# GLA values taken token by token, with the first adaLN block behind them

## The chip, the cores and the metric

The kernel runs on one core of one Trainium2 chip. The metric is the device time of one execution in microseconds; several runs are taken and their median is given. A profile is one execution recorded by the hardware profiler: its span goes from the first to the last instruction of that execution, and its rows name lines of the kernel (L863 is line 863).

The engines are called by their names and by the short forms of the profile: TensorE (PE for its matmuls, PEld for its weight loads), VectorE (DVE), ScalarE (ACT), GpSimd (POOL) and SyncE (SP), which issues most transfers.

## The reference, cut to what matters

The program is one step of a two-layer model on 512 latent tokens and 128 context tokens, 640 in all, with 1024 features. Layer 0 mixes tokens by gated linear attention (GLA) with 4 heads, layer 1 by differential attention; a SwiGLU block follows each. What the change touches is in the GLA layer:

```
z = h @ w_in                       # h: 640 x 1024
q, k                               # 128 columns a head
v, r                               # 256 columns a head
la_f, la_b = gates of the two directions
for each direction: chunks of 64 tokens
    b = cumsum(log decay);  q_d = q*exp(b);  k_d = k*exp(-b);  k_end = k*exp(b_last - b)
    A = mask(q_d k_d^T);  dS = k_end^T v;  S = decay*S + dS
    o = A v + q_d S
o = rmsnorm(o_f + o_b) * silu(r);  x += gate * (o @ w_out)
```

Shift, scale and gate of each sublayer come from `silu(c) @ w_ada` (adaLN), 12 blocks of 512 columns a layer, which the kernel computes between other work.

## The kernel before, in words

All activations lie feature by partition: h is stored as 8 tiles of 128 features by 640 tokens, split in two parts, h_hi and h_lo, in a rounded 32-bit format (fp32r). Each weight matrix is loaded in tiles of 1024 rows by 128 columns into w_raw (two slots), then ScalarE rounds it into w_hi (`split_hi`, L1606) and VectorE takes the rest into w_lo (`split_lo`, L2443). A product is three passes: w_hi by h_hi, w_hi by h_lo, w_lo by h_hi. `tile_products` (L863) does this for one tile of 128 features: the weight tile is the stationary operand, and the 640 tokens move in two halves of 320.

A **unit** is one weight tile of 128 columns, 8 x 3 x 2 = 48 matmuls. A GLA head has six: u = 0 (q), 1 (k), 2 and 3 (the two halves of v), 4 and 5 (the two halves of r). All six accumulate in acc[0], two PSUM banks, and ScalarE reads each out (`unit_read`, L1746) before the next may begin; the counters acc_free say so. Units 2 and 3 leave the values as v_t, features by tokens. The chunk products need them with tokens on the partitions, so TensorE turns v_t in five 128 x 128 pieces per unit (`v_turn`, through `five`, L1030), and VectorE copies the turned tiles into v_tok (`v_copy`, L2667).

Everything else in the stage stands **between** units on TensorE, in an order written out by hand in `gla_period`, once per head p with the tail of head p - 1. It uses a ring of three PSUM buffers (work, side, acc[1]); the list GLA_RING gives the order of the turns, and a turn waits until the buffer's use three turns earlier has been read (`gla_begin`). The turns are: Z0, Z1 gate products (L1021); KE0, KE1 the turned k_end (L1030); A0, A1 the scores (L1040); DB, DF, DX the chunk sums (L1067); Oa, Ob the outputs (L1082, L1086); OT0, OT1 the turned outputs; AD0, AD1, AD2 the adaLN blocks of the head (16 matmuls of 512 columns, L898).

ScalarE, VectorE and POOL have `gla_period` lists of their own, each a strict queue. On VectorE the end of the list for a head reads: gate logarithms (L2594), scan of direction 1 (L2604), `gla_ada(p, 0)` (adds the adaLN block to a_row, L2751 or L2754; it waits for the block's matmuls), scan of direction 0, k_d of direction 1 (L2624). The list of the head then begins with k_end of direction 1 (zb, L2633), k_d of direction 0, the variance of the head before (L2712), q_d of direction 1 (L2614), w_lo of unit 4. On ScalarE, the stretch is: w_hi of unit 4, the exponentials of the two directions (`decays`, L1737 and L1738, each direction after its scan), the logarithm for the output norm of the head before (L1809, with a table load; it waits for the variance), the read of unit 3, and the exponential of the norm (L1815).

Of the kernel before, what the change touches and what calls it, by code (L numbers as in the profile page):

```python
# [20 lines left out]
P = 128  # L21
# [52 lines left out]
def program(nc, x_prompt, x_sample, state_f, state_b, cache_k, cache_v, c, c_ctx, w_ada, b_ada, g_mix, g_ffn,  # L74
# [3 lines left out]
    with ctx:  # L78
# [111 lines left out]
        v_t = take("v_t", [P, T])  # L190
# [277 lines left out]
        def cols(w, col, kt=KD):  # L468
            return w.rearrange("(k p) n -> p k n", p=P)[:, 0:kt, col]
# [30 lines left out]
        def state_out(d, n):  # L500
            if n >= SCH:
# [10 lines left out]
        GLA_RING = [("Z0", 0), ("Z1", 0), ("Oa", -1), ("AD2", -1), ("Ob", -1), ("AD0", 0), ("VT0", 0), ("KE1", 0),  # L512
                    ("A1", 0), ("VT1", 0), ("OT0", -1), ("KE0", 0), ("AD1", 0), ("DB0", 0), ("DB1", 0), ("DF0", 0),
                    ("A0", 0), ("OT1", -1), ("DF1", 0), ("DX", 0)]
        GLA_END = {name: b for name, b in (("AD3", 0), ("OT0", 0), ("OT1", 1), ("AT", 1))}
        gla_turns = [(name, p + off) for p in range(GH + 1) for name, off in GLA_RING if 0 <= p + off < GH]
        gla_turns = [(name, h) for name, h in gla_turns if h < GH - 1 or name not in GLA_END]
        gla_place, gla_total, gla_made = {}, [0] * NB, [0] * NB
        for i, turn in enumerate(gla_turns + [(name, GH - 1) for name in GLA_END]):
            b = i % NB if i < len(gla_turns) else GLA_END[turn[0]]  # L520
            summed = turn[0] in ("AD0", "AD1", "AD2", "AD3", "AT")
            gla_place[turn] = (b, gla_total[b], gla_made[b])
            gla_total[b] += 1
            gla_made[b] += 0 if summed else 1
# [81 lines left out]
        def _(sp):  # L606
# [7 lines left out]

            sp.dma_start(x_in[:, 0:NS // P, :], x_sample[0].rearrange("(t p) d -> p t d", p=P)).then_inc(x_land, 16)
# [34 lines left out]
            def gla_head(h, first=False):  # L650
                if not first:
                    load(3 * h, 0, cols(w_in0, bass.ds(h * P, P)))
                    load(3 * h, 1, cols(w_in0, bass.ds(512 + h * P, P)))
                load(3 * h + 1, 0, cols(w_in0, bass.ds(1024 + h * DV, P)))
                load(3 * h + 1, 1, cols(w_in0, bass.ds(1024 + P + h * DV, P)))
                load(3 * h + 2, 0, cols(w_in0, bass.ds(2048 + h * DV, P)))
                load(3 * h + 2, 1, cols(w_in0, bass.ds(2048 + P + h * DV, P)))
# [198 lines left out]
        def _(pe):  # L856
# [193 lines left out]
            def v_turn(h, j):  # L1050
                if not gla_live(h):
                    return
                pe.wait_ge(acc_free[j], 3 * h + 2)
                five(h, f"VT{j}", lambda t: v_t[:, t * P:(t + 1) * P])

            def kv_sums(h, name):
                if not gla_live(h):
                    return
                for d in range(2):
                    if any(d == part for part, _ in KV[name]):  # L1060
                        pe.wait_ge(*gla_freed(h, f"KE{d}"))
                for j in range(2):
                    pe.wait_ge(*gla_freed(h, f"VT{j}"))
# [38 lines left out]
            def gla_unit(h, u, a, b):  # L1102
# [3 lines left out]
                if a == 0:  # L1106
                    pe.wait_ge(lo_ready, unit(pair, slot) + 1)
                    pe.wait_ge(acc_free[1 - slot], pair + slot)
                for k in range(a, b):
# [32 lines left out]
            def gla_period(p):  # L1142
# [7 lines left out]
                gla_unit(p, 2, 0, 8)  # L1150
                gla_ada(p, 0)
                gla_unit(p, 3, 0, 2)
                v_turn(p, 0)
                gla_unit(p, 3, 2, 6)
                k_end_turn(p, 1)
                gla_unit(p, 3, 6, 8)
                scores(p, 1)
                gla_unit(p, 4, 0, 5)
                v_turn(p, 1)
                gla_unit(p, 4, 5, 8)  # L1160
# [439 lines left out]
        def _(act):  # L1600
# [164 lines left out]
            def v_read(h, j):  # L1765
                if not gla_live(h):
                    return
                if j:
                    act.wait_ge(*gla_done(h, "VT0"))
                elif h:  # L1770
                    act.wait_ge(*gla_done(h - 1, "VT1"))
                unit_read(h, 2 + j, v_t[:, :], ACT.Copy)
# [49 lines left out]
            def gla_period(p):  # L1822
# [15 lines left out]
                v_read(p, 0)  # L1838
# [4 lines left out]
                v_read(p, 1)  # L1843
# [595 lines left out]
        def _(dve):  # L2439
# [220 lines left out]
            def v_copy(h, j):  # L2660
                if not gla_live(h):
                    return
                dve.wait_ge(*gla_done(h, f"VT{j}"))
                if h:
                    for name in ("DF0", "DF1", "DB0", "DB1", "DX", "Oa", "Ob"):
                        dve.wait_ge(*gla_done(h - 1, name))
                dve.tensor_copy(v_tok[:, :, j * P:(j + 1) * P],  # L2667
                                gla_buf(h, f"VT{j}")[:, 0:T].rearrange("p (t n) -> p t n", t=NT))\
                    .then_inc(gla_freed(h, f"VT{j}")[0], 1)

# [99 lines left out]
            def gla_period(p):  # L2770
# [5 lines left out]
                v_copy(p, 0)  # L2776
# [5 lines left out]
                v_copy(p, 1)  # L2782
# [832 lines left out]
```

## Time and profile before

| | |
|---|---|
| median of 3 runs | 1644.24 us (1641.31 to 1644.34) |
| the profiled execution | 1646.1 us, of which the span is 1644.3 us |
| mean granted TensorE clock | 0.991 of full speed |
| TensorE matmuls | 1606.0 us busy, 98% of the span, 11252 instructions |
| TensorE weight loads | 1517.3 us, 92% |
| VectorE | 1174.8 us, 71% |
| ScalarE | 820.7 us, 50% |
| POOL | 96.5 us, 6% |
| chain that ended last | 93% TensorE, of it 43% of the span in L863 |
| transfers | 171.09 MB, 104 GB/s mean |

A matmul's busy time runs from its start to its modelled end, and matmuls overlap, so its price is the distance between two starts, not its duration. A row of the time line gives start, duration, engine, line, operation, the tiles it writes and reads (moving operand first), the shape and the number of merged instructions; in brackets the idle time ahead of it and what ended it. The GLA stage lies between 45 and 325 us of the span; heads 0 to 3 begin at about 51, 107, 173 and 239 us.

### The profile page before, as it was taken

What the parts mean: (1) busy time and instruction counts of PE and PEld (TensorE: products, weight loads), DVE (VectorE), ACT (ScalarE), POOL (GpSimd) and SP (SyncE); (2) the same over time, 40 slices, a digit from 0 to 9 for tenths busy, and PEclk for the clock granted to TensorE, in tenths of its full rate; (3) what the DMA queues carried; (4) which work ended last, traced back from release to release, by engine and by line L of the source; (5) the groups of instructions that cost most, each with busy time, mean ns of one, the idle gap of its engine ahead of it and who ended that gap; (6) DMA issues with size and microseconds to landing.
All of it is one profiled execution on the core that took longest, in us unless ns stands there. A gap on an engine that the chain in (4) does not pass through costs nothing.

```text
span 1644.3 us, 28912 instructions
## 1 busy us (share of the span) xinstructions
PE 1606.0 (98%) x11252; PEld 1517.3 (92%) x11252; DVE 1174.8 (71%) x2049; ACT 820.7 (50%) x1448; POOL 96.5 (6%) x145
## 2 busy tenths in 40 slices
PE   6999999999999999999999999998999999999998
PEld 3888888799999999999989999998899999999998
DVE  5546455689758758667767887787898587586776
ACT  4634535366524425334547777776565254253445
POOL 1211101200100000000000000000000000000000
PEclk9999999999999999999999999999999999999999
DMA  9545445632532423323322222223222232232312
GB/s 325 162 131 177 132 139 167 203 86 78 158 96 83 129 75 103 108 86 99 104 66 76 65 73 66 65 63 116 63 78 71 84 93 76 65 102 65 103 41 88
DMA packets 230395, 171.09 MB, mean 104 GB/s; under 512 B 10643, under 2 KB 210998, under 8 KB 230262
## 3 DMA queue, kind: packets, MB, share of 16 engines
q1 hardware_dynamic: 216470, 121.42, 25.5%
q0 software_dynamic: 13792, 47.85, 8.6%
q8 instruction: 90, 1.47, 0.4%
q14 instruction: 43, 0.35, 0.1%
HBM read 160.32 MB, written 4.72 MB: 100 GB/s over the span
## 4 chain that ended last, share of the span: by engine, by line
PE 93%; DVE 3%; ACT 1%; issue 1%; DMA 1%; SPq 0%; DVEq 0%; ACTq 0%
PE acc L863 43%; PE acc L1244 28%; PE side L1244 5%; PE side L1424 2%; PE side L1469 1%; PE acc L1469 1%; PE side L898 1%; PE work L1398 1%; PE acc L1551 1%; PE acc L898 1%; DVE x L2821 1%; PE work L950 0%; PE work L1086 0%; PE work L898 0%; PE acc L1119 0%
## 5 line engine op out<-in xcount | busy, mean ns | idle before, releaser
L863 PE MATMUL acc<-h_hi,w_hi 128*128 128x320 f32 x1006 | 242.6, 323 | 6.4 <-issue 2.2
L863 PE MATMUL acc<-h_lo,w_hi 128*128 128x320 f32 x1006 | 231.4, 311 | 0.0
L863 PE MATMUL acc<-h_hi,w_lo 128*128 128x320 f32 x1006 | 230.6, 311 | 0.0
L863 PEld LDWEIGHTS acc<-h_hi,w_hi 128*128 128x128 f32 x1006 | 165.8, 190 | 30.1 <-issue 19.9
L1244 PE MATMUL acc<-ax_hi,ff_hi 128*128 128x322 f32 x528 | 166.2, 315 | 5.0 <-issue 3.2
L863 PEld LDWEIGHTS acc<-h_lo,w_hi 128*128 128x128 f32 x1006 | 170.6, 190 | 0.0
L863 PEld LDWEIGHTS acc<-h_hi,w_lo 128*128 128x128 f32 x1006 | 170.5, 190 | 0.0
L2821 DVE SCALAR_TENSOR_TENSOR x<-acc,mods,x 128x320 f32<-128x320 f32 (+2 forms) x231 | 87.2, 433 | 114.1 <-PE acc L863 113.8
L1244 PE MATMUL acc<-h_hi,w_hi 128*128 128x322 f32 x616 | 167.2, 313 | 0.1
L1244 PE MATMUL acc<-ax_hi,ff_lo 128*128 128x322 f32 x528 | 164.8, 312 | 0.0
L1244 PE MATMUL acc<-ax_lo,ff_hi 128*128 128x322 f32 x528 | 164.7, 312 | 0.0
L1244 PE MATMUL acc<-h_lo,w_hi 128*128 128x322 f32 x440 | 137.4, 312 | 0.0
L863 PE MATMUL acc<-hid_hi,ff_hi 128*128 128x320 f32 x566 | 129.0, 309 | 0.0
L863 PE MATMUL acc<-hid_hi,ff_lo 128*128 128x320 f32 x566 | 129.0, 309 | 0.0
L863 PE MATMUL acc<-hid_lo,ff_hi 128*128 128x320 f32 x566 | 128.9, 309 | 0.0
L2443 DVE TENSOR_TENSOR w_lo<-w_raw,w_hi 128x1024 fp32r<-128x1024 f32 (+2 forms) x66 | 78.3, 1187 | 67.8 <-ACT w_hi L1606 67.6
L1244 PE MATMUL acc<-h_hi,w_lo 128*128 128x322 f32 x440 | 121.2, 310 | 0.0
L1244 PEld LDWEIGHTS acc<-h_hi,w_hi 128*128 128x128 f32 x616 | 110.7, 189 | 1.0 <-issue 0.6
L1244 PEld LDWEIGHTS acc<-ax_hi,ff_hi 128*128 128x128 f32 x528 | 100.3, 190 | 10.3 <-issue 7.8
L1244 PEld LDWEIGHTS acc<-ax_lo,ff_hi 128*128 128x128 f32 x528 | 100.5, 190 | 0.2
L1244 PEld LDWEIGHTS acc<-ax_hi,ff_lo 128*128 128x128 f32 x528 | 99.9, 189 | 0.0
L1922 ACT ACTIVATE w_hi<-ff_sum 128x512 fp32r<-128x512 f32 x88 | 55.1, 626 | 85.6 <-PE acc L1244 41.9
(478 smaller groups left out, 3662.0 us busy)
## 6 DMA issues: line engine op xcount, KB each, us to landing
a_raw<-in_w_ada_dram POOLq DMA_DIRECT2D x80, 512.0 KB, 6.2
ff_raw<-in_w_ffn_gate_dram SPq DMA_DIRECT2D x88, 256.0 KB, 3.3
ff_raw<-in_w_ffn_up_dram SPq DMA_DIRECT2D x88, 256.0 KB, 4.2
w_raw<-in_w_gla_in_dram SPq DMA_DIRECT2D x24, 512.0 KB, 3.7
ff_raw<-in_w_ffn_down_dram SPq DMA_DIRECT2D x32, 384.0 KB, 3.5
w_raw<-in_w_diff_qkv_dram SPq DMA_DIRECT2D x24, 512.0 KB, 4.0
ff_raw<-in_w_ffn_down_dram SPq DMA_DIRECT2D x32, 320.0 KB, 3.2
a_left<-in_w_ada_dram SPq DMA_DIRECT2D x8, 512.0 KB, 9.6
```

The costliest lines, as they stand in the source:

```text
L863: mm = pe.matmul(out[:, s, 0:HALF + s * more], w[:, k * P:(k + 1) * P], a(k)[:, s * HALF:(s + 1) * HALF + s * more], start=(k == 0 and n = ...
L898: mm = pe.matmul(out[q * CG:(q + 1) * CG, 0:512], cond_at(2 * q + j, place), a_raw[q][:, j, :], start=(b == lo and j == 0), stop=(b == hi ...
L1244: mm = pe.matmul(out, w[:, j * P:(j + 1) * P], x_part, start=(name in ("P1", "P7", "P2") and j == 0 and n == 0), stop=(j == JT - 1 and n = ...
L1398: mm = pe.transpose(out[:, t * P:(t + 1) * P], tile, ident[:, :])
L1424: mm = pe.matmul(outs[m], qq[h % 2][rows, cols], kk[h % 2][rows, keys], start=(n == 0), stop=(n == 2))
L1469: mm = pe.matmul(out[:, 0:2 * P], vv[h % 2][:, t, :], wt[pp][:, t, :], start=(t == 0), stop=(t == SK // P - 1))
L1551: mm = pe.matmul(tail_acc(g, u), w[:, k * P:(k + 1) * P], h[:, k, a:b], start=(k == 0 and m == 0), stop=(k == kt - 1 and m == 2))
L1922: act.activation(ff_slot(i, name)[0], ff_source(i, name), ACT.Copy).then_inc(ff_high, 1)
L2443: dve.tensor_tensor(w_lo[slot][:, 0:kt * P], w_raw[slot][:, 0:kt * P], w_hi[slot][:, 0:kt * P].bitcast(F32), ALU.subtract).then_inc(lo_rea ...
L2821: op = dve.scalar_tensor_tensor(out=xk[:, lo:hi], in0=src[:, half, lo - half * HALF:hi - half * HALF], scalar=mods[:, one, v], in1=xk[:, l ...
```

## The change

The two value units become two halves of one product with the operands exchanged: a tile of h (128 features by 128 tokens) is the stationary operand and 256 weight columns move. The result has tokens on its partitions, so v_t, the turns of v and their copies are gone. A half now is 4 of the 8 feature tiles with all 256 columns, and each half is 4 x 5 x 3 = 60 matmuls. Token tiles 0 to 3 accumulate in acc[0], tile 4 in a new turn of the ring, V4. ScalarE reads all three pieces into v_tok after the second half, in the place where it read unit 3. On TensorE the adaLN block AD0 stood between the two value units and now stands behind both, followed by the turn of k_end of direction 1 and the scores, which stood inside and behind unit 3. The ring's list changes with it, and the last period gets a list of its own. VectorE's list loses the two copies and is otherwise as it was.

```diff
-        GLA_RING = [("Z0", 0), ("Z1", 0), ("Oa", -1), ("AD2", -1), ("Ob", -1), ("AD0", 0), ("VT0", 0), ("KE1", 0),
-                    ("A1", 0), ("VT1", 0), ("OT0", -1), ("KE0", 0), ("AD1", 0), ("DB0", 0), ("DB1", 0), ("DF0", 0),
+        GLA_RING = [("Z0", 0), ("Z1", 0), ("Oa", -1), ("AD2", -1), ("Ob", -1), ("V4", 0), ("AD0", 0), ("KE1", 0),
+                    ("A1", 0), ("OT0", -1), ("KE0", 0), ("AD1", 0), ("DB0", 0), ("DB1", 0), ("DF0", 0),
                     ("A0", 0), ("OT1", -1), ("DF1", 0), ("DX", 0)]
...
+        LAST_RING = [("AD2", -1), ("Oa", -1), ("Ob", -1)]
...
+            def load_values(pair, slot, col):
+                sp.wait_ge(lo_ready, unit(pair, slot) - 1)
+                half = w_in0.rearrange("(s k p) n -> p s k n", s=2, p=P)[:, slot, :, col]
+                sp.dma_start(w_raw[slot][:, :].rearrange("p (k n) -> p k n", k=KD // 2), half).then_inc(raw_in[slot], 16)
...
-            def v_turn(h, j):
+            def values_by_token(h, half):
                 if not gla_live(h):
                     return
-                pe.wait_ge(acc_free[j], 3 * h + 2)
-                five(h, f"VT{j}", lambda t: v_t[:, t * P:(t + 1) * P])
+                pair = 3 * h + 1
+                pe.wait_ge(lo_ready, unit(pair, half) + 1)
+                if half == 0:
+                    pe.wait_ge(acc_free[1], pair)
+                    gla_begin(h, "V4")
+                outs = [acc[0][:, t // 2, t % 2 * DV:t % 2 * DV + DV] for t in range(NT - 1)] + [gla_buf(h, "V4")[:, 0:DV]]
+                for j in range(KD // 2):
+                    k = KD // 2 * half + j
+                    w = slice(j * DV, (j + 1) * DV)
+                    for t, out in enumerate(outs):
+                        for n, (a, part) in enumerate(((h_hi, w_hi), (h_hi, w_lo), (h_lo, w_hi))):
+                            mm = pe.matmul(out, a[:, k, t * P:(t + 1) * P], part[half][:, w],
+                                           start=(k == 0 and n == 0 and t in (0, 2, 4)), stop=(k == KD - 1 and n == 2),
+                                           skip_group_check=True)
+                mm.then_inc(unit_mm, 1)
...
@@ TensorE, gla_period
-                gla_unit(p, 2, 0, 8)
+                values_by_token(p, 0)
+                values_by_token(p, 1)
                 gla_ada(p, 0)
-                gla_unit(p, 3, 0, 2)
-                v_turn(p, 0)
-                gla_unit(p, 3, 2, 6)
                 k_end_turn(p, 1)
-                gla_unit(p, 3, 6, 8)
                 scores(p, 1)
-                gla_unit(p, 4, 0, 5)
-                v_turn(p, 1)
-                gla_unit(p, 4, 5, 8)
+                gla_unit(p, 4, 0, 8)
...
@@ ScalarE
-            def v_read(h, j):
+            def v_read(h):
...
+                act.wait_ge(unit_mm, 6 * h + 4)
+                if h:
+                    for name in ("DF0", "DF1", "DB0", "DB1", "DX", "Oa", "Ob"):
+                        act.wait_ge(*gla_done(h - 1, name))
+                for j in range(2):
+                    act.activation(v_tok[:, 2 * j:2 * j + 2, :].rearrange("p t n -> p (t n)"), acc[0][:, j, :], ACT.Copy)\
+                        .then_inc(acc_free[j], 1)
+                act.activation(v_tok[:, NT - 1, :], gla_buf(h, "V4")[:, 0:DV], ACT.Copy).then_inc(gla_freed(h, "V4")[0], 1)
...
                 gate_log(p, 1)
-                v_read(p, 0)
                 unit_split(p, 4)
                 decays(p, 1)
                 decays(p, 0)
                 o_log(p - 1)
-                v_read(p, 1)
+                v_read(p)
                 o_exp(p - 1)
...
@@ VectorE, gla_period
                 unit_split(p, 4)
-                v_copy(p, 0)
                 k_ended(p, 0)
                 q_decayed(p, 0)
                 masked(p, 1)
                 o_norm(p - 1)
                 unit_split(p, 5)
-                v_copy(p, 1)
```

Two waits follow the new buffers: unit 4 waits for both halves of acc[0] to be read, and the chunk sums wait for the read of acc[0] and of V4. By the new list the scores A1 stand three turns behind V4 and use its buffer.

## Rows read from the trace of the kernel before

**Rows 1.** What TensorE waited for, whole run: total us, times, longest.

```profile
PE acc L1244 <- issue: 3.2, 2, 2.5
...
PE side L898 <- DVE state L2691: 1.6, 1, 1.6
```

**Rows 2.** TensorE in order of time in head 1.

```profile
134.80 0.56 PE L863 MATMUL acc<-h_hi,w_hi 128*128 128x320 f32 x2
...
136.67 0.71 PE L1030 MATMUL work<-ident,v_t 128*128 128x128 f32 x5
...
137.51 0.46 PE L863 MATMUL acc<-h_lo,w_hi 128*128 128x320 f32 x2
...
140.43 0.45 PE L863 MATMUL acc<-h_hi,w_lo 128*128 128x320 f32 x2
...
143.03 1.27 PE L1040 MATMUL acc<-q_d,k_d 128*128 128x128 f32 x10
144.14 0.53 PE L863 MATMUL acc<-h_hi,w_hi 128*128 128x320 f32 x2
```

**Rows 3.** VectorE in order of time in head 1.

```profile
134.94 0.69 DVE L2754 TENSOR_TENSOR a_row<-a_row,acc 128x512 f32<-128x512 f32 x1 [2.29 <-PE acc L898]
135.54 1.48 DVE L2604 TENSOR_TENSOR_SCAN zb<-chunk_mask,za 128x640 f32<-128x640 f32 x1
137.47 0.83 DVE L2624 TENSOR_TENSOR k_d<-k_t,zb 128x640 f32<-128x640 f32 x1 [0.45 <-ACT zb L1738]
...
138.43 0.82 DVE L2633 TENSOR_TENSOR zb<-k_d,decay 128x640 f32<-128x640 f32 x1
139.17 0.82 DVE L2624 TENSOR_TENSOR k_d<-k_t,zb 128x640 f32<-128x640 f32 x1
...
140.06 0.82 DVE L2614 SCALAR_TENSOR_TENSOR q_d<-q_t,za 128x640 f32<-128x640 f32 x1
140.79 1.22 DVE L2443 TENSOR_TENSOR w_lo<-w_raw,w_hi 128x1024 fp32r<-128x1024 f32 x1
```

**Rows 4.** ScalarE in order of time in head 1.

```profile
137.97 0.72 ACT L1738 ACTIVATE zb<-zb 128x640 f32<-128x640 f32 x1
138.71 1.28 ACT L1809 ACT_TABLE_LOAD   x1
```

**Rows 5.** TensorE in the last down projection: the first and last of nine.

```profile
1624.51 0.28 PE L1551 MATMUL acc<-hid_hi,h_hi 128*128 128x256 f32 x1
...
1625.46 0.28 PE L1551 MATMUL acc<-hid_hi,h_lo 128*128 128x256 f32 x1
```

**Rows 6.** Instructions of a_row: ns shortest/median/longest, first and last start.

```profile
L1667 ACT ACTIVATE a_row<-side x2: 577/578/578, 827.1 to 1220.3; 128x512 f32<-128x512 f32 x2
```

**Rows 7.** Head 0 in order of time: VectorE's a_row, TensorE's start of unit 4.

```profile
69.75 0.69 DVE L2751 COPY a_row<-acc 128x512 f32<-128x512 f32 x1 [2.59 <-PE acc L898]
...
78.95 0.53 PE L863 MATMUL acc<-h_hi,w_hi 128*128 128x320 f32 x2
```

**Rows 8.** The end of head 3: the last states on VectorE, the first output on TensorE.

```profile
302.36 0.87 DVE L2691 SCALAR_TENSOR_TENSOR state<-state,decay,acc 128x256 f32<-128x256 f32 x2
...
304.02 0.61 PE L1082 MATMUL work<-v_tok,attn 128*32 128x256 f32 x8
```

**Rows 9.** Windows of 1 us: length, TensorE busy (count), granted clock, DMA share, GB/s.

```profile
28.00:29.00 1.00, 0.23 (x1) 0.62 1.05 387
...
35.00:36.00 1.00, 1.00 (x10) 0.97 0.17 32
...
1120.00:1121.00 1.00, 0.69 (x3) 0.75 0.74 210
...
1123.00:1124.00 1.00, 1.00 (x6) 0.54 0.97 339
...
1195.00:1196.00 1.00, 0.68 (x3) 0.80 0.00 0
...
1202.00:1203.00 1.00, 1.00 (x5) 0.79 0.00 0
```

More of the change, by code:

```diff
@@ L189, in program @@
         k_t = take("k_t", [P, T])
-        v_t = take("v_t", [P, T])
         v_tok = take("v_tok", [P, NT, DV])
@@ L511, in program @@
         NB = len(bufs)
-        GLA_RING = [("Z0", 0), ("Z1", 0), ("Oa", -1), ("AD2", -1), ("Ob", -1), ("AD0", 0), ("VT0", 0), ("KE1", 0),
-                    ("A1", 0), ("VT1", 0), ("OT0", -1), ("KE0", 0), ("AD1", 0), ("DB0", 0), ("DB1", 0), ("DF0", 0),
+        GLA_RING = [("Z0", 0), ("Z1", 0), ("Oa", -1), ("AD2", -1), ("Ob", -1), ("V4", 0), ("AD0", 0), ("KE1", 0),
+                    ("A1", 0), ("OT0", -1), ("KE0", 0), ("AD1", 0), ("DB0", 0), ("DB1", 0), ("DF0", 0),
                     ("A0", 0), ("OT1", -1), ("DF1", 0), ("DX", 0)]
         GLA_END = {name: b for name, b in (("AD3", 0), ("OT0", 0), ("OT1", 1), ("AT", 1))}
-        gla_turns = [(name, p + off) for p in range(GH + 1) for name, off in GLA_RING if 0 <= p + off < GH]
+        LAST_RING = [("AD2", -1), ("Oa", -1), ("Ob", -1)]
+        gla_turns = [(name, p + off) for p in range(GH + 1) for name, off in (GLA_RING if p < GH else LAST_RING)
+                     if 0 <= p + off < GH]
         gla_turns = [(name, h) for name, h in gla_turns if h < GH - 1 or name not in GLA_END]
@@ L520, in program @@
             b = i % NB if i < len(gla_turns) else GLA_END[turn[0]]
-            summed = turn[0] in ("AD0", "AD1", "AD2", "AD3", "AT")
+            summed = turn[0] in ("AD0", "AD1", "AD2", "AD3", "AT", "V4")
             gla_place[turn] = (b, gla_total[b], gla_made[b])
@@ L653, in gla_head @@
                     load(3 * h, 1, cols(w_in0, bass.ds(512 + h * P, P)))
-                load(3 * h + 1, 0, cols(w_in0, bass.ds(1024 + h * DV, P)))
-                load(3 * h + 1, 1, cols(w_in0, bass.ds(1024 + P + h * DV, P)))
+                for s in range(2):
+                    load_values(3 * h + 1, s, bass.ds(1024 + h * DV, DV))
                 load(3 * h + 2, 0, cols(w_in0, bass.ds(2048 + h * DV, P)))
@@ L1062, in kv_sums @@
                 for j in range(2):
-                    pe.wait_ge(*gla_freed(h, f"VT{j}"))
+                    pe.wait_ge(acc_free[j], 3 * h + 2)
+                pe.wait_ge(*gla_freed(h, "V4"))
                 out = gla_begin(h, name)
@@ L1108, in gla_unit @@
                     pe.wait_ge(acc_free[1 - slot], pair + slot)
+                    if u == 4:
+                        pe.wait_ge(acc_free[0], pair)
                 for k in range(a, b):
@@ L1763, in k_read @@
                 unit_read(h, 1, k_t[:, :], ACT.Copy)
-            def v_read(h, j):
+            def v_read(h):
                 if not gla_live(h):
                     return
[L1768 to L1772, printed above, removed]
+                act.wait_ge(unit_mm, 6 * h + 4)
[6 more added lines that the diff above has]
+                act.activation(v_tok[:, NT - 1, :], gla_buf(h, "V4")[:, 0:DV], ACT.Copy).then_inc(gla_freed(h, "V4")[0], 1)
             def r_read(h, j):
@@ L2658, in mask_sum @@
                 dve.tensor_tensor(attn[:, :], attn[:, :], zb[1][:, :], ALU.add).then_inc(attn_ready, 1)
[L2660 to L2669, printed above, removed]
             def states(h, name):
```

## The prediction

> **What bounds the kernel now.** I read first where TensorE waits [rows 1]. Two rows are to be seen: after the start of the program no wait is longer than 2.5 us, and the longest in the whole GLA stage (45 to 325 us) is one of 1.6 us, for a state update on VectorE at its end. So the stage is a gap-free TensorE program: each microsecond added to or taken from that program moves the end, and work on the other engines is free as long as its result is there when TensorE comes to it. How much slack those results have is what decides here.
>
> Second, TensorE in order of time in head 1 [rows 2]. The rows are the restart after the adaLN block (134.80), a turn of v (136.67), two later pairs, the scores (143.03) and the start of unit 4 (144.14). Third, the same stretch on VectorE [rows 3] and ScalarE [rows 4]. The thing to see there is one row: at 134.94 VectorE starts a_row, after 2.29 us of waiting for the adaLN matmuls (L898), and straight behind it in its queue stand the scan of direction 0, k_d, zb (k_end of direction 1), k_d of direction 0 and q_d of direction 1.
>
> **The value products themselves.** Old: 96 matmuls of 320 columns. From 137.51 to 140.43 are 10 pairs, 0.146 us a matmul [rows 2], so 14.02 us a head. New: 120 of 256 columns. The trace has this form in the last down projection: nine from 1624.51 on, the ninth at 1625.46, 0.119 us each [rows 5], each with its own 128-column load. That makes 14.26 us, +0.24 a head. The bounds: 0.117 (the columns alone, 256/320 of 0.146), and 0.146 if a matmul with its load can't be spaced closer than the old ones; I take the tail's rows, since they are the same form and type. The Trainium skill (TensorE: Matmul & The Clock Gate, section Back-to-back issue gap) has sustained spacings of about 81 ns at 128 and 131 ns at 512 columns, which would make more and shorter matmuls dearer; interpolated (an estimate from that page) they give +1.5 us a head, +6 in all, where the rows give +1.0.
>
> **What is removed.** Two turns of v: 136.67 to 137.51 is 0.84 where a pair takes 0.29, so 0.55 us each on TensorE [rows 2], 1.1 a head. The k_end turn now stands behind the adaLN block and not inside a unit, and two restarts of the stream fall away, which I take as 0.08 each (in [rows 2] the pair of a restart is 0.53 to 0.56 long and one within the stream 0.45 or 0.46). On ScalarE two reads of 0.70 become three (two of 512 columns, 0.58 each by the same form [rows 6], and one of 256, which I take as 0.4), on VectorE two copies of 0.8 go; both are beside TensorE. Left alone these would give -1.0 us a head. The loads of the weights keep size, place and queue, with 1 KB runs where there were 512 B; nothing waits for them in this stage, and I cost them at nothing.
>
> **What is moved.** The first adaLN block goes behind the second value half. VectorE's order isn't changed with it: a_row still stands ahead of the scan. TensorE reaches the block later by 7.25 us (60 x 0.119 and the 0.12 by which the first half is longer than unit 2). In head 1 that is:
> - TensorE is through the block at 134.80 + 7.25 = 142.05 and next wants the k_end turn of direction 1.
> - a_row starts at 142.19, the scan 0.60 later, ending at 144.27; k_d of direction 1 follows, zb 0.96 behind it (145.2) and ends at 146.05 [rows 3]. TensorE idles 4.0 us, then turns for 0.46.
> - k_d of direction 0 at 146.0, q_d of direction 1 0.89 later, to 147.7: the scores can't start before that. w_lo of unit 4 follows q_d, to 148.8.
> - On ScalarE the two exponentials of direction 0 need that scan (144.3), 1.35 us together, then the table load of 1.28 and the logarithm: 147.1. Only then does it reach the new read of the values [rows 4]: three copies, 1.4 us with their overlap, to 148.5. The scores now take the PSUM buffer of the fifth value tile, so they wait for the last of them; 148.6.
> - Scores 1.11, unit 4 starts at 149.7, against 144.14 [rows 2]: +5.56. The second turn of v is gone from unit 4: **+5.0 us** for each of heads 1, 2 and 3.
>
> Head 0 has no logarithm of a head before. Its a_row moves from 69.75 to 77.0, q_d ends 5.5 later (82.5), w_lo at 83.6 and the scores too; unit 4 starts at 83.7 against 78.95 [rows 7]: +4.75, less 0.55, **+4.2**. Behind unit 4 everything has seven more microseconds of cover (o_norm, the split of unit 5, the k_end reads) and I cost it at nothing. POOL's load of the next adaLN block starts 7 us later too; it had 18 us until its use, and 16 remain for transfers of about 6.
>
> At the end of head 3 the third adaLN block gets the buffer of a turn long read, and doesn't wait for the states. The last state update ends at 303.23, so the outputs can start at 303.35 and not at 304.02 [rows 8]: -0.65. Sum without the clock: 3 x 5.0 + 4.2 - 0.65 = **+18.5**.
>
> **The clock.** The new stall leaves TensorE 6.1 us idle of 6.6 in a head that had none. Three times the trace of before shows the granted clock going from the 2.4 to the 1.2 GHz level, each time in or just behind a stretch in which TensorE waited [rows 9]: low from 28.24 to 35.06 (busy from 28.77 on), from 1120.5 to 1123.9, and from 1195.6 to 1202.4 (0.6 of it idle). Work at the low level takes twice as long, so they cost 3.1, 1.7 and 3.1 us. No wait there is longer than 2.5 us [rows 1], and I expect 4.0 and 2.1 us almost back to back, so I take a fall in each head, at the mean of the three: 2.65, 10.6 for four. From below it is 0, from above 3.4 a head, 13.6. The Trainium skill (same page, section Why this matters for your kernels) says that an idle gap between bursts of matmuls puts the array back to half rate. By that rule all four heads fall, by its absence the time is that of the second rival below; the three rows agree with it.
>
> **Sum:** +29. The profiled execution took 1646.1 us (span 1644.3), 1.9 above the median of the runs; it would go to 1675, the median from 1644.2 to **1673**.
>
> **The rivals.**
> - *The block behind the values holds nobody up.* If the a_row addition did not hold the scan (another order on VectorE, or ada_mm counted so that it is let through), only the removals stay: 4 x -1.03 - 0.65 = -4.8, **1639.4**, faster. It decides at one point: whether VectorE's scan of direction 0 is done before TensorE ends the values. For it speaks only that the wait costs nothing today, as 2.29 us of it are VectorE's own idle time; against it the order of the rows on VectorE, which the change leaves. 4%.
> - *The stall, with the clock up.* The turns between the two waits might keep it up, or the falls end before TensorE is back. 1644.2 + 18.5 = **1663**. No row shows a wait of 4 us, from which the rest would follow; the three falls speak against it. 14%.
> - *The stall, and the new matmuls no closer than the old* (0.146 each): 120 x 0.027 = 3.2 a head, 13, **1686**. Against it stand the tail's rows. The page's spacings named above point this way. 4%.
> - *The stall is partly covered or has a second part*: the scores wait only for q_d and not for the value copies (0.9 less a head), or unit 5 gets a wait of its own. 1669 or 1677, inside the range.
>
> **How the numbers follow.** Forecast with a fall in each head, 76%, by itself 1668 to 1678 (2.0 to 3.4 us a fall and a microsecond a head on the chain's lags). The rest of the chance goes to the rivals as given, 2% to a stall of which half is hidden. The range takes in the case with the clock up, 1661 to 1681. About 0.2% (3.3 us) is what a measurement can tell from no change here; all cases but the first rival lie well above it: faster 4%, same 1%, slower 95%.
>
> **What would show it.** Right: in VectorE's waits an idle time of some 9 us ahead of a_row in each head; TensorE waiting 4 us for zb and about 2 us for ScalarE's value read (or q_d) ahead of the scores, four times; granted clock at the low level for some microseconds in each unit 4; matmuls of 256 columns 0.119 apart; no wait of the adaLN block for the state at the end. Wrong: no wait on L1030 or L1040 in the GLA stage, or rows with a full clock through all four unit 4s.

## The result, and the profile of the changed kernel

The changed kernel takes 1670.8 us (median of 4 runs, 1670.4 to 1671.6), the one before 1644.2 beside it: a ratio of 1.0165, 95% interval 1.0153 to 1.0177. It is 26.6 us slower; 1673 was forecast, in a range of 1661 to 1681. The profiled execution spans 1669.0 us, 24.7 more than that of before.

Where TensorE waited between 45 and 400 us (total us, times, longest). In the kernel before, the longest here was 1.6 us [rows 1]; now four waits of some 4 us for zb lead the list, and a second kind stands behind them, for ScalarE's read of the values:

```profile
PE side L1037 <- DVE zb L2653: 8.0, 2, 4.1
PE acc L1037 <- DVE zb L2653: 3.9, 1, 3.9
PE work L1037 <- DVE zb L2653: 3.9, 1, 3.9
PE acc L1047 <- ACT v_tok L1793: 1.9, 1, 1.9
PE work L1047 <- ACT v_tok L1793: 1.3, 1, 1.3
PE side L1047 <- ACT v_tok L1793: 1.3, 1, 1.3
PE work L1103 <- DVE state L2700: 1.0, 1, 1.0
```

One wait is spread over several rows, because the program's result buffers (acc, side, work) take turns from head to head. Added up by line they are four waits for zb, 15.8 us, and three for the read, 4.5 us. The fourth head is head 0: its scores start 0.27 us behind the turn's end, when q_d is ready (VectorE ends it at 81.83, they start at 81.93).

TensorE in order of time in head 1, the values' first and last products, the adaLN block, the turn of k_end, the scores, and the first pairs of unit 4 (answers to [rows 2]; start, duration, in brackets the idle time before):

```profile
130.74 0.39 PE L1071 MATMUL acc<-w_hi,h_hi 128*128 128x256 f32 x1
...
144.88 0.28 PE L1071 MATMUL side<-w_hi,h_lo 128*128 128x256 f32 x1
145.09 1.92 PE L905 MATMUL acc<-a_raw,cond 128*32 128x512 f32 x16
150.88 1.33 PE L1037 MATMUL work<-ident,zb 128*128 128x128 f32 x5 [3.87 <-DVE zb L2653]
153.56 2.47 PE L1047 MATMUL side<-q_d,k_d 128*128 128x128 f32 x10 [1.35 <-ACT v_tok L1793]
155.68 0.88 PE L870 MATMUL acc<-h_hi,w_hi 128*128 128x320 f32 x2
156.36 0.65 PE L870 MATMUL acc<-h_lo,w_hi 128*128 128x320 f32 x2
156.85 0.45 PE L870 MATMUL acc<-h_hi,w_lo 128*128 128x320 f32 x2
```

The 120 value products take 144.88 - 130.74 = 14.14 us to the start of the last, 0.119 apart. The five turns last 1.33 us and the ten score products 2.47, where their like in direction 0 of the same trace, at the full clock, last 0.71 and 1.27. The pairs of unit 4 start at 0.88 and are back to 0.45 by the third.

VectorE and ScalarE behind it (answers to [rows 3] and [rows 4]):

```profile
147.08 0.69 DVE L2763 TENSOR_TENSOR a_row<-a_row,acc 128x512 f32<-128x512 f32 x1 [9.41 <-PE acc L905]
147.69 1.48 DVE L2624 TENSOR_TENSOR_SCAN zb<-chunk_mask,za 128x640 f32<-128x640 f32 x1
150.00 0.82 DVE L2653 TENSOR_TENSOR zb<-k_d,decay 128x640 f32<-128x640 f32 x1
151.63 0.81 DVE L2634 SCALAR_TENSOR_TENSOR q_d<-q_t,za 128x640 f32<-128x640 f32 x1
```
```profile
149.20 0.74 ACT L1755 ACTIVATE za<-zb 128x640 f32<-128x640 f32 x1 [7.25 <-DVE zb L2624]
150.58 1.28 ACT L1830 ACT_TABLE_LOAD   x1
152.05 1.09 ACT L1791 ACTIVATE v_tok<-acc 128x512 f32<-128x512 f32 x2
153.02 0.39 ACT L1793 ACTIVATE v_tok<-side 128x256 f32<-128x256 f32 x1
```

VectorE stands idle for 9.41 us with a_row at the head of its queue (2.29 before, [rows 3]); all that follows it is late by that, and through the scan ScalarE too, which idles for 7.25. Windows of 1 us in head 1 (length, TensorE busy, granted clock, DMA share, GB/s), answering to [rows 9]:

```profile
149.00:150.00 1.00, 0.00 (x0) 0.98 0.91 201
150.00:151.00 1.00, 0.12 (x1) 0.50 0.91 332
152.00:153.00 1.00, 0.21 (x1) 0.50 1.05 328
154.00:155.00 1.00, 1.00 (x7) 0.50 0.98 379
156.00:157.00 1.00, 1.00 (x7) 0.61 0.98 277
157.00:158.00 1.00, 1.00 (x9) 1.00 0.32 94
```

The clock falls to the 1.2 GHz level at 150.0, while TensorE waits for zb, and is back at 156.8. It falls in all four heads, for 6.8 us each: from 78.3 to 85.1, 150.0 to 156.8, 225.1 to 231.9 and 296.7 to 303.6. In heads 0, 1 and 3 it falls in the wait for zb. In head 2 the turn of k_end still runs at the full clock (0.77 us), and the fall comes in the wait behind it:

```profile
223.61 0.77 PE L1037 MATMUL side<-ident,zb 128*128 128x128 f32 x5 [3.87 <-DVE zb L2653]
226.29 2.47 PE L1047 MATMUL acc<-q_d,k_d 128*128 128x128 f32 x10 [1.91 <-ACT v_tok L1793]
```

The last columns of the windows are worth keeping in mind: the DMA engines are full from 149 to 157. They carry the weights of the second adaLN block, issued from 147.66 on (2.10 MB between 147 and 165), and beside them two tiles of unit weights (1.05 MB).

The end of the stage (answers to [rows 8]):

```profile
326.14 1.92 PE L905 MATMUL acc<-a_raw,cond 128*32 128x512 f32 x16
329.06 0.64 PE L1103 MATMUL work<-v_tok,attn 128*32 128x256 f32 x8 [1.00 <-DVE state L2700]
```

The first output of head 3 starts at 329.06 against 304.02: +25.0, or +25.6 if each is counted from the first value product of head 0 (60.00 and 60.56). The whole spans differ by 24.7, so the difference arises in this stage.

### The profile page after: what moved, and what is told of

Its sections match the earlier page's. It is cut to its first block, busy times and chain, and to the rows that moved or that the text cites. A ratio compares the mean times of both kernels' runs of the same rounds, so it can differ in the third digit from the quotient of the medians.

```text
span 1669.0 us, 28993 instructions
## 1 busy us (share of the span) xinstructions
PE 1609.7 (96%) x11308; PEld 1520.3 (91%) x11308; DVE 1167.8 (70%) x2041; ACT 821.1 (49%) x1452; POOL 96.5 (6%) x145
## 4 chain that ended last, share of the span: by engine, by line
PE 89%; DVE 6%; ACT 3%; issue 2%; DMA 1%; SPq 0%; ACTq 0%; DVEq 0%
PE acc L870 39%; PE acc L1262 26%; PE side L1262 4%; PE acc L1071 3%; PE side L1442 2%; PE side L1487 1%; PE acc L1487 1%; PE side L905 1%; PE work L1416 1%; PE acc L1569 1%; DVE x L2828 1%; PE work L905 0%; PE acc L1047 0%; PE acc L1142 0%; PE work L1442 0%
## 5 line engine op out<-in xcount | busy, mean ns | idle before, releaser
L870 PE MATMUL acc<-h_hi,w_hi 128*128 128x320 f32 x878 | 213.1, 324 | 5.7 <-DVE h_lo L2529 1.9
L870 PE MATMUL acc<-h_lo,w_hi 128*128 128x320 f32 x878 | 203.0, 313 | 0.0
L870 PE MATMUL acc<-h_hi,w_lo 128*128 128x320 f32 x878 | 201.4, 311 | 0.0
L870 PEld LDWEIGHTS acc<-h_hi,w_hi 128*128 128x128 f32 x878 | 146.3, 192 | 24.2 <-issue 14.2
L870 PEld LDWEIGHTS acc<-h_lo,w_hi 128*128 128x128 f32 x878 | 150.0, 192 | 0.0
L870 PEld LDWEIGHTS acc<-h_hi,w_lo 128*128 128x128 f32 x878 | 149.4, 191 | 0.0
L2463 DVE TENSOR_TENSOR w_lo<-w_raw,w_hi 128x1024 fp32r<-128x1024 f32 (+2 forms) x66 | 78.3, 1187 | 67.4 <-ACT w_hi L1624 67.2
L1262 PEld LDWEIGHTS acc<-h_hi,w_hi 128*128 128x128 f32 x616 | 110.7, 189 | 3.5 <-DVE ff_lo L2894 2.1
```

The lines of the kernel that those rows point to most:

```text
L870: mm = pe.matmul(out[:, s, 0:HALF + s * more], w[:, k * P:(k + 1) * P], a(k)[:, s * HALF:(s + 1) * HALF + s * more], start=(k == 0 and n = ...
L1262: mm = pe.matmul(out, w[:, j * P:(j + 1) * P], x_part, start=(name in ("P1", "P7", "P2") and j == 0 and n == 0), stop=(j == JT - 1 and n = ...
L2463: dve.tensor_tensor(w_lo[slot][:, 0:kt * P], w_raw[slot][:, 0:kt * P], w_hi[slot][:, 0:kt * P].bitcast(F32), ALU.subtract).then_inc(lo_rea ...
```

## The experiments

The stall could come from where the block stands, from the form of the products, or from both. The first three runs take these apart.

**1. The add behind what it holds up.** Only VectorE's order is edited:

```
@@ VectorE, gla_period(p)
                 q_decayed(p, 1)
                 unit_split(p, 4)
+                gla_ada(p, 0)
                 k_ended(p, 0)
...
                 scan(p + 1, 1)
-                gla_ada(p + 1, 0)
                 scan(p + 1, 0)
```

> The changed kernel with one edit on VectorE: the addition of the first adaLN block to a_row stands behind q_d and w_lo of unit 4, and no longer ahead of the scan of direction 0. Theory (the addition holds VectorE's queue until TensorE has done the block): both new waits on TensorE go, for zb (3.9 to 4.1 us a head) and for the value read (1.3 to 1.9), the granted clock stays up in heads 0 to 3, and the time is that of the removals alone, 1644.2 - 4.8 = 1639.4 us, 1637 to 1642. Rival A (the new value read on ScalarE, or the scores' new buffer, is what holds TensorE): the wait for zb goes but one of 1 us or more ahead of the scores stays, about 1648 to 1652. Rival B (the new form of the value products is itself dearer): over 1650 with no wait in the stage.

Measured: 1646.2 us, ratio 1.0014 (1.0005 to 1.0023). Of the 26.6 us, 24.6 are gone: one line in VectorE's queue was the cause. The clock stays up through the stage. But the 1639.4 of the first rival did not come either, nor the 1637 to 1642 expected here. TensorE's waits from 45 to 400 us have neither zb nor v_tok, and a new kind:

```profile
PE side L905 <- DMA a_raw<-in_w_ada_dram: 3.0, 2, 1.8
PE acc L905 <- DMA a_raw<-in_w_ada_dram: 1.4, 1, 1.4
PE work L905 <- DMA a_raw<-in_w_ada_dram: 1.0, 1, 1.0
```

The second adaLN block now waits for its weights, 5.4 us in four heads, which is most of the 6.8 missing. POOL and TensorE of this run in head 1:

```profile
141.97 2.88 POOL L779 DMA_DIRECT2D a_raw<-in_w_ada_dram  x4 [19.68 <-PE acc L905]
```
```profile
153.08 1.92 PE L905 MATMUL side<-a_raw,cond 128*32 128x512 f32 x16 [1.80 <-DMA a_raw<-in_w_ada_dram]
```

The four loads can be issued only when the first block has been multiplied (they share its buffers), and the last of them is there 11.1 us after the first is issued (141.97 to 153.08; 10.2 to 10.8 in the other heads). In the kernel before, 17.5 us lay between the first issue and the use of the block (135.51 to 152.99). With the first block 7 us later, the turn of v gone from unit 4 and no stall, it is 9.3: TensorE wants the block at 151.28. In the changed kernel as it stands, the stall itself covers the loads (147.66 to 164.47), which is why no trace of it shows this wait.

**2. The block back between the halves.** The new products stay, the block goes where it was, a half of the values earlier:

```
@@ TensorE, gla_period(p)
                 values_by_token(p, 0)
+                gla_ada(p, 0)
                 values_by_token(p, 1)
-                gla_ada(p, 0)
                 k_end_turn(p, 1)
```

> The changed kernel with one edit on TensorE: the first adaLN block stands between the two value halves, as it stood between the two value units; VectorE as in the changed kernel. Theory: the wait for zb goes and the clock stays up; but only the turn of k_end (0.46 us) now lies between the last value product and the scores, and the read of the values takes ScalarE 1.5 us, so TensorE waits about 1.1 us a head for it, at 16.3 + 1.5 against 16.8 us behind the start of the values: +4.4 on 1639.4, 1643 to 1645 us, no difference from before. Rival A (the place of the block doesn't matter, the value read does): 1665 or more. Rival B (the form is dearer): over 1650 with no wait.

Measured: 1644.6, ratio 1.0005 (0.9996 to 1.0014), as expected; the clock stays up. What is left:

```profile
PE acc L1047 <- ACT v_tok L1793: 2.0, 2, 1.0
PE side L1047 <- ACT v_tok L1793: 1.0, 1, 1.0
PE work L1047 <- ACT v_tok L1793: 1.0, 1, 1.0
```

The products' own gain (about a microsecond a head) is given back by a microsecond of waiting, since the fifth value tile lies in the buffer that the scores want.

**3. The old products, the block moved.** The kernel before, with the block behind its second value unit:

```
@@ TensorE, gla_period(p)
-                gla_ada(p, 0)
                 gla_unit(p, 3, 0, 2)
                 v_turn(p, 0)
-                gla_unit(p, 3, 2, 6)
+                gla_unit(p, 3, 2, 8)
+                gla_ada(p, 0)
                 k_end_turn(p, 1)
-                gla_unit(p, 3, 6, 8)
                 scores(p, 1)
```

In the ring's list VT0 stands ahead of AD0 with it.

> The kernel before, with values by feature and their turns, and only the first adaLN block moved behind unit 3, followed by the turn of k_end and the scores (the ring's list with VT0 ahead of AD0). Theory: the same stall without any new form or new read: unit 4 starts some 6.5 to 7.5 us later in each head (the scores also wait for the copy of the first turned value half, whose buffer they take), the clock falls in each head for 1.5 to 3 us of loss, 1672 to 1681 us. Rival A or B (the stall comes from the new read or form): within 3 us of the kernel before, 1641 to 1648.

Measured: 1684.8, ratio 1.0242 (1.0226 to 1.0258), 4 us above the range. The stall is there without the new form, and its first wait has the same size. Besides it there is a wait that was not expected: unit 3 waits for ScalarE's read of unit 2, which the block between them had covered in the kernel before:

```profile
PE acc L863 <- ACT v_t L1745: 3.7, 4, 0.9
```
```profile
156.71 0.77 PE L1030 MATMUL side<-ident,zb 128*128 128x128 f32 x5 [3.87 <-DVE zb L2632]
160.29 2.48 PE L1040 MATMUL acc<-q_d,k_d 128*128 128x128 f32 x10 [2.81 <-DVE v_tok L2666]
```

Here the copy of the turned values is on VectorE, in the same late queue, and the second wait is 2.2 to 2.8 us; the clock is at the low level for 34 us of the stage against 27 in the changed kernel. The 3.7 us of waits for unit 2's read are about what the range was missed by. So the position alone makes a stall at least as large as the one seen; the changed kernel has no such waits, shorter second waits, and loses 14 us less.

**4. The first wait filled.** To price the clock apart from the stall, 26 matmuls without use run while TensorE would wait for zb:

```
@@ TensorE
+            def fill_wait(h):
+                if not gla_live(h):
+                    return
+                out = gla_begin(h, "KE1")
+                for n in range(26):
+                    pe.matmul(out[:, 0:HALF], h_hi[:, n % KD, 0:P], h_hi[:, n % KD, 0:HALF], start=True, stop=True)
...
                 gla_ada(p, 0)
+                fill_wait(p)
                 k_end_turn(p, 1)
```

> The changed kernel with 26 more matmuls of 320 columns in each head, into the free buffer that the turn of k_end takes next, between the adaLN block and that turn. Their results are overwritten. They take 26 x 0.146 = 3.8 us of the 3.9 to 4.1 that TensorE waits there. Theory of the clock (the low level costs 7.5 us: the scores 1.0 longer in each head and 0.5, 0.5, 1.7 and 0.7 in unit 4): work in the place of the wait keeps the clock up, and the time falls by 7.5, to 1663, 1661 to 1666 us, with scores of 1.1 us. Rival (the low level costs nothing that counts, or falls all the same from the second wait): 1669 to 1672 us.

Measured: 1666.4, ratio 1.0127 (1.0112 to 1.0143), just above the range. The wait for zb is filled (the turn starts 5.79 us behind the block, as in the changed kernel), and in heads 0 and 2 the clock stayed up. In heads 1 and 3 it fell behind the second wait instead, which had grown from 1.35 us to 1.91, since the turns now run at full speed and end earlier while the read does not:

```profile
149.29 0.77 PE L1037 MATMUL work<-ident,zb 128*128 128x128 f32 x5
151.97 1.53 PE L1047 MATMUL side<-q_d,k_d 128*128 128x128 f32 x10 [1.91 <-ACT v_tok L1801]
```

Low from 153.0 to 156.4 and from 296.4 to 299.8: 6.8 us in all with TensorE busy, so half of it, 3.4, is lost. Less that it would be 1663.0, the figure of the second rival (an estimate: the profile is of one execution, of 1666.9 us). The fastest of the four took 1662.6 at a mean granted clock of 0.994, where the others have 0.992; that would fit an execution without these two falls, but its trace is not on record.

**5. The read of the values ahead of the logarithm.**

```
@@ ScalarE, gla_period(p)
-                o_log(p - 1)
                 v_read(p)
+                o_log(p - 1)
                 o_exp(p - 1)
```

> The changed kernel with one edit on ScalarE: the three reads of the values stand ahead of the logarithm of the head before and its table load, and not behind them. Theory: the first wait (zb, 3.9 to 4.1 us a head) stays as it is; the second one is then set by q_d on VectorE and not by the value read, the scores of heads 1 to 3 start 0.9 us sooner, head 0 is unchanged: 2.7 us, 1668 us, 1665 to 1670. Rival A (the value read behind ScalarE's queue is the main stall): down by 15 us or more, under 1656.

Measured: 1667.5, ratio 1.0142 (1.0125 to 1.0159), 3.3 us under the changed kernel, as expected. The profiled executions are 4.6 apart, in two parts: from the turn to the scores it is 1.0 us less in each of heads 1 to 3, and the clock was low for 20.5 us and not 27.3, 3.1 less of it behind the start of the scores, where it costs half. The scores now wait for q_d, as the prediction's fourth rival has it:

```profile
151.67 2.47 PE L1047 MATMUL side<-q_d,k_d 128*128 128x128 f32 x10 [0.34 <-DVE q_d L2634]
```

**6. The second block later.** This goes after the wait that the first run brought up: from there, the second block is moved behind the kv sums and into unit 5, and the turn of k_end into unit 4 (with the order of the result buffers and of VectorE's adds to match):

```
@@ TensorE, gla_period(p), from run 1
-                gla_unit(p, 4, 0, 8)
+                gla_unit(p, 4, 0, 5)
+                k_end_turn(p, 0)
+                gla_unit(p, 4, 5, 8)
                 o_turn(p - 1, 0)
-                k_end_turn(p, 0)
-                gla_ada(p, 1)
                 kv_sums(p, "DB0")
                 kv_sums(p, "DB1")
                 kv_sums(p, "DF0")
                 gla_unit(p, 5, 0, 4)
+                gla_ada(p, 1)
                 scores(p, 0)
```

> The values token by token, VectorE's add of the first adaLN block behind q_d and unit 4 as in the first run, and besides that the second adaLN block moved on TensorE from behind unit 4 to the middle of unit 5, behind the three kv sums (6.4 us later: 2.8 of kv sums and 3.5 of half a unit), with k_end's second turn brought forward into unit 4. Theory (what held the first run at the time of before was the second block's wait for its weights, 5.4 us in four heads, since the four loads of 512 KB are issued once the first block is multiplied and need about 10 us): that wait is gone, no wait takes its place, and the time is 5 us under the first run, 1639.5 to 1641.5 us, faster than before by 0.2 to 0.3%. Rival (the 10 us are not the transfers' own time but contention with the unit's weights, so that a later use finds them later still): the wait on the DMA remains at over 2 us in all and the time stays over 1643. Second rival (the turn of k_end in the middle of unit 4 comes before its operand or the kv sums before its read): a wait of about 1 us a head on zb or k_end, about 1644.

Measured: 1643.7, ratio 0.9995 (0.9986 to 1.0004): 2.5 us under the first run and not 5, outside the range. Heads 0 to 2 are as the theory has them, without a wait: the first blocks of heads 1, 2 and 3 start at 138.80, 204.16 and 269.51, a period of 65.36 us, where before has 66.26 (132.95 to 199.21). But in head 3 the third block stands close behind the second and waits for its weights, and the clock falls with it, from 299.8 to 303.2:

```profile
287.83 1.92 PE L905 MATMUL work<-a_raw,cond 128*32 128x512 f32 x16
...
299.79 3.57 PE L905 MATMUL acc<-a_raw,cond 128*32 128x512 f32 x16 [3.17 <-DMA a_raw<-in_w_ada_dram]
```

The second expectation of the same theory (no wait takes its place) fell; the wait had moved on one block. Both numbers of the first rival came, over 2 us of DMA wait (3.2) and a time over 1643, though not where it had them: the later use in heads 0 to 2 found the weights there.

**7. The scores into unit 4.** The second run with two of unit 4's eight steps ahead of the scores:

```
@@ TensorE, gla_period(p), from run 2
-                scores(p, 1)
-                gla_unit(p, 4, 0, 8)
+                gla_unit(p, 4, 0, 2)
+                scores(p, 1)
+                gla_unit(p, 4, 2, 8)
```

> The second run (block between the halves of the values) with the scores of the first half moved two of eight steps into unit 4 on TensorE (1.76 us later). Its trace has one new wait, 1.0 us a head, of the scores for the read of the values by ScalarE. Theory: these 4.0 us are all that keeps that kernel at the time of before, so that it comes to 1640.5 us (1639.5 to 1642), 0.2% faster than before, and the wait on the read is gone from the page. Rival: what stands behind the scores (the mask, o_norm, kv sums) is pushed by 1.76 us and a wait of 0.5 to 1 us a head comes up elsewhere (on VectorE's k_end, o_gate or states, or on the second block's weights), 1643 to 1645.

Measured: 1643.3, ratio 0.9993 (0.9984 to 1.0002): 1.3 us gained, not 4, and inside the range of the rival (1643 to 1645). The wait on the read is not gone, it changed its line and went from 4.0 us to 2.7:

```profile
PE acc L870 <- ACT v_tok L1792: 2.7, 4, 0.7
```

Unit 4 writes where the first four value tiles lie, so it wants the read as much as the scores do. I had freed the scores of a wait that stood ahead of both.

**8. The third block of the last head later.** The answer tried for the sixth run's wait: outputs, then two steps of the first output unit, then the block (with the ring's last turns and VectorE's add to match).

```
@@ TensorE, behind the last period, from run 6
-            gla_ada(h, 2)
             outputs(h, 0)
             outputs(h, 1)
-            first_out(0, 0, KD - 2)
+            first_out(0, 0, 2)
+            gla_ada(h, 2)
+            first_out(0, 2, KD - 2)
```

> The sixth run with the third adaLN block of the last head moved on TensorE behind both outputs and two of eight steps of the first output unit (5.0 us later), and VectorE's add of it behind the two copies of o. In the sixth run that block was the only one to wait for its weights (3.2 us at 296.6, 12 us after the loads could be issued), and the clock was low for some 2 us behind it. Theory (that wait and the clock behind it, 3.2 and 0.6, are what kept the sixth run at the time of before): the wait is gone and the time is 3 to 4 us under the sixth run, 1640.0 (1639 to 1641.5). Rival (the fourth block, 9.5 us behind the third, becomes the late one): it waits 1 to 3 us for its weights and the time is 1641.5 to 1643.5. Second rival: fast and slow order of the transfers only moves the wait on, 1643.7 as the sixth.

Measured: 1652.0, ratio 1.0044 (1.0030 to 1.0057), 8.4 us worse than the sixth run. This missed on every count:

```profile
PE work L905 <- DMA a_raw<-in_w_ada_dram: 6.0, 1, 6.0
PE acc L1103 <- DVE state L2702: 2.9, 1, 2.9
```

The third block had been the cover for the last state update, which the outputs now wait for with TensorE idle; and the fourth block waits 6.0 for its weights, twice what the rival named. It starts 11.7 us behind the third (309.11 to 320.77), about the distance that the sixth run has from second to third (12.0): the loads take their time from wherever they are issued, and the order had left them 3.7 (311.03 to 314.75). The clock was low for 10.2 us behind the two waits, where the sixth run has 3.4.

**9. First wait filled, read first.** The edits of the fourth and the fifth run together:

```
@@ TensorE, gla_period(p)
                 gla_ada(p, 0)
+                fill_wait(p)
                 k_end_turn(p, 1)
@@ ScalarE, gla_period(p)
-                o_log(p - 1)
                 v_read(p)
+                o_log(p - 1)
```

> The changed kernel with TensorE's first wait of each head filled by 26 matmuls without use, as in the fourth run, and ScalarE's read of the values ahead of its logarithm, as in the fifth. No low clock should be left between 60 and 305 us: the wait before the scores shrinks from 1.9 (for the read) to 0.9 (for q_d, whose end is set by VectorE's order and does not move). Theory (stall and clock are separate terms, of which the clock is worth about 7.5 us in the four heads): 1659.6 to 1661, that is 1644.2 + 15.8 of filled time + 3.6 of waits for q_d - 4.1 of cheaper values = 1659.5, or the fourth run less 4.1 of wait and 2 of clock = 1660.3. Rival (10.6 us of clock, as predicted, with the stall smaller): 1657 or below. Second rival (the clock falls behind 0.9 us of waiting too): a low clock in some head and 1662 to 1664.

Measured: 1660.8, ratio 1.0097 (1.0081 to 1.0112), inside the range. No window between 60 and 350 us has a low clock; the scores wait for q_d, 0.9 us:

```profile
151.21 1.35 PE L1047 MATMUL side<-q_d,k_d 128*128 128x128 f32 x10 [0.90 <-DVE q_d L2642]
```

So the stall by itself, with the clock up and the read out of the way, still leaves the kernel 16.8 us slower.

**10. The last head's cover kept.** The sixth run in heads 0 to 2; in head 3 the second block stands where the first run has it:

```
@@ TensorE, gla_period(p), from run 6
                 o_turn(p - 1, 0)
+                if p == GH - 1:
+                    gla_ada(p, 1)
                 kv_sums(p, "DB0")
...
                 gla_unit(p, 5, 0, 4)
-                gla_ada(p, 1)
+                if p < GH - 1:
+                    gla_ada(p, 1)
```

VectorE's adds and the ring's list for head 3 go with it.

> The sixth run in heads 0 to 2 (period of 65.36 us against 66.26 in before), and in head 3 the second adaLN block back between the turn of o and the first kv sum, as in the first run, so that the third block's loads are issued about 5 us earlier again. Theory (each block wants 12 to 13 us behind the one before it; the sixth run's 3.2 us wait and the low clock behind it are gone, and the eighth run's 2.9 for the state, that only the third block covered, does not come back, since that block keeps its place): head 3 waits 1.0 us for the second block's weights and 1.0 for the state, as in the first run, and from the first value matmul of head 0 to the outputs of head 3 it takes 194.9 + 45.2 = 240.1 us against 243.5 in before, so 1641.0 us (1640 to 1642.3), 0.2% faster than before. Rival (the time is moved on into a later wait behind 305 us once more): 1643 to 1646.

Measured: 1641.4, ratio 0.9982 (0.9973 to 0.9991), inside the range and a little faster than both kernels; the clock stays up. What is left between 45 and 400 us:

```profile
PE work L908 <- DMA a_raw<-in_w_ada_dram: 1.3, 1, 1.3
PE work L1106 <- DVE state L2707: 1.0, 1, 1.0
```

The 0.18% are just under what I said a measurement tells from no change, but the interval of these 11 runs excludes one.

## Why the prediction was right, and where it was not

*The value products.* 0.119 us each, as taken from the tail. 120 of them take 14.26 us (14.14 to the start of the last). The spacings that the Trainium skill gives (TensorE: Matmul & The Clock Gate, section Back-to-back issue gap; 81 ns at 128 columns and 131 at 512) are not borne out: interpolated, an estimate from that page, they are 0.098 us at 256 columns and 0.106 at 320, where the traces have 0.119 and 0.146, and the +1.5 us a head worked out from them is far above the +0.24 of the measured spacings. With no wait at all a head is 0.91 us shorter (run 6), which has one more restart inside a unit than the changed kernel's order; 1.03 was forecast.

*The stall.* The steps hold one by one:

| step in head 1 | predicted | in the trace |
|---|---|---|
| the block later by | 7.25 | 7.16 from the first product (14.35 against 7.19) |
| wait for zb | 4.0 | 3.87 |
| scores held by, heads 1 to 3 | the read of the values | the same |
| unit 4 against before | +5.56 | +6.56 (24.94 against 18.38), 1.02 of it the slow scores |

The table counts from the first value product (125.76 and 130.74). In head 0 the scores wait for q_d and unit 4 is later by 5.67, where 4.75 and the slow scores make 5.77. At the end of head 3 the third block does not wait for the state; the outputs do, for 1.00 us, and come 17.95 us behind the second block and not 18.48: 0.5 of the 0.65. Over the four heads it is +25.6 up to the outputs, and taking away the clock's share (below) leaves 18.1 for the stall, where 18.5 was the sum. That the position of the block ahead of VectorE's add does it, and not the form of the products, is shown by runs 1 to 3.

*The clock* is the term of the sum that was mis-sized: 10.6 was taken, four times the mean of three earlier falls. In each head the clock was low for 6.8 us, as long as the longest of those. But 1.2 to 2.3 us of that TensorE was waiting, and a wait costs the same at either level. The turns at half speed in heads 0, 1 and 3 cost nothing either, since the scores were held by others: in run 4, with the turns at full speed, they start just as long behind the turn (2.68 us in head 1, 1.59 in head 0). That leaves 3.2, 3.2, 5.6 and 3.5 us of work at the low level. What counts is the scores (1.02 us more each, 2.12 to the next start in head 1 against 1.11) and the head of unit 4, 0.5, 0.5, 1.7 and 0.7 us: about 7.5 in all. Taking a price per fall from falls that hit a busy engine was the error; it has to be read against where the falling clock meets the wait. Two runs agree, by estimates of the same kind: run 4 and 3.4 us of remaining loss taken away gives 1663.0, so 7.8 for the clock; run 9 plus its shorter second wait (3.5 us in four heads, against 6.5 in run 4) gives 1663.8, so 7.0. With 7.5 in place of 10.6 the sum is 1670.2; measured is 1670.8.

The forecast's fourth rival (scores held by q_d alone) was a true alternative and needed one more edit, run 5. The second rival's condition was made in part by run 4; its 1663 is what is left when the two remaining falls are taken off, and was not measured as a median. The third's condition did not occur.

*The first rival's price* was wrong, and with it a step of the forecast that happened not to matter: "it had 18 us until its use, and 16 remain for transfers of about 6". The 6 us are what the profile's list of DMA issues gives for one of the four loads (6.2 us median of 80 in the kernel before). Four of 512 KB are issued over 2.9 us and share the engines with a unit's weights; the last is there 9.4 us (run 8: issued from 311.37, used from 320.77) to 11.1 us (run 1) after the first is issued. And the 16 us (16.8 in the trace) count the stall. Take the stall away and 9.3 are left. So 1639.4 was never to be had by VectorE's order alone: 1646.2 was. With the loads' time respected (run 10) it is 1641.4, with 2.3 us of waiting still to be seen.

*Open:* why the clock fell behind a wait of 1.9 us in heads 1 and 3 of run 4 and not in head 2, whose wait was as long, nor behind the 1.8 of run 1. And how much of the 9.4 to 11.1 us is the four loads' own and how much they lose to the unit weights that move beside them: no run took those away.

## What to carry to other kernels

When a block of work moves on one engine, look for its consumer's place in another engine's in-order queue: an add of 0.69 us that nobody was waiting for cost 25 us here, because the scan behind it fed two engines, and the clock fell in the stall. A result's move also moves the release of its buffers, and a stall can hide what that costs, so price the repaired order as well as the broken one, counting until the last of a group of loads has landed and not one of them. And where every block of a chain covers something (a state update, the next block's weights), moving one of them moves the wait on, as in runs 6 and 8; in run 7 the wait for a read moved on in the same way. Only an order that kept 13 us or more from the start of one block to the next and the last head's cover in its place paid off, by 0.2% (run 10).

## What the runs showed of the hardware

- A fall of the clock costs far less than its length where it falls together with waits: 27 us at the low level in four heads cost about 7.5 (7.0 to 7.8 by runs 4 and 9), not 13.6.
- Waits of 0.9 us in each head left the clock up (run 9), and so did 1.0 to 1.8 (run 1). It fell in two heads of three with one of 1.9 (run 4), and in four of four with one of 3.9 to 4.1 followed by another of 0.3 to 1.9 (changed kernel, run 5).
- Four weight loads of 512 KB took 9.4 to 11.1 us from the first issue to their use, where TensorE stood waiting for them (runs 1, 6, 8 and 10), though the list of issues gives a median of 6.1 to 6.8 us for one.
- The fp32r products with a 128-column load of their own run 0.119 us apart at 256 columns and 0.146 at 320, so about in proportion to the columns moved.
